# Modulation weights loaded as 64 rows by two column blocks, one partition sum per vector, and x loaded in quarters

## The chip, the cores and the metric

One core of a Trainium2 chip runs the whole program. The metric is the device time of one execution in microseconds. TensorE (PE) multiplies and transposes; VectorE (DVE), ScalarE (ACT) and GpSimd (POOL) do the rest; SyncE (SP) issues nearly all loads, which run on 16 DMA engines.

## The reference

x is 256 tokens by 1024 channels, all in float32. It goes through an encoder of two layers and then two layers of a second block, whose normalised inputs are modulated by vectors that depend on one conditioning vector c:

```python
c_silu = jax.nn.silu(c)
for layer in range(DEPTH):                                    # 2
    mods = jnp.split(c_silu @ ada_w[layer] + ada_b[layer], 9, axis=-1)
    h = modulate(rms_norm(x, norm_g[layer, 0]), mods[0], mods[1])
    x = x + 0.5 * (1 + mods[2]) * swiglu(h, ffn_w_in[layer, 0], ffn_w_out[layer, 0])
    ... # pool mixer or block attention with mods[3..5]
```

Before it, first_block: twice rmsnorm, projection w_in (1024 to 4096), neighbourhood and differential attention, gates, projection w_out, and the final norm. So there are 20 modulation vectors of 1024 (9 + 2 + 9), each the product of c_silu (1024) with a 1024x1024 slice of weights: 20 x 4 MB to be read, for one row of result each.

## The kernel before

**Weights.** The weights of the projections are cut into 189 units of 1 MB (128 partitions x 2048), in the order of use. SP loads a unit into raw (ring of RAW = 6), once unit u - 6 is used. ACT rounds it to w_hi (L647, ring of 4), DVE (L1164) or POOL (L516) computes w_lo = raw - w_hi, and PE makes three products, w_hi with the high and the low part of the activations (L1831, L1836) and w_lo with the high part (L1844), for either half t of the tokens. A step of one unit and one token half (half_step) is 12 matmuls of 512 columns. PE runs its queue in order; a step of it waits for w_hi, then for the low activations, then for w_lo.

**Modulation vectors.** They aren't made on PE's product path. A list, ada_after, fixes behind which weight unit each of N_ADA = 160 slots of 512 KB is loaded (L482) into ada_raw (ring of ADA_RING = 4); SP waits at L475 to L481 for a free slot, so the next weight unit stands behind it. DVE multiplies each 128x512 part by its column of c_silu (ccol) and adds it up (L1143, L1150, function ada, two per slot). A slot is 256 rows (2 per partition) of a 512-column half of one vector, so 4 slots make a half vector in ada_acc: a partial sum in each of 128 partitions. ada_sum (L1858) transposes it on PE in 4 blocks, and reduce_vector on DVE (L1108) sums over the free dimension; with the second half it adds the bias and finishes the vector (scale times gain, and the like). Where a sum stands is computed: in the encoder by SUM_STEPS (steps of a layer's w_in product), later behind a weight unit (sum_unit), away from two QUIET stretches; one half vector is put into the pool stage (in_pool).

**The start.** SP issues x's first token half (512 KB), the two halves of unit 0, x's second half, units 1 to 3, seven small constants, then unit 4. ACT issues the identity and the norm gains; PE, DVE and ACT all wait for both (first_in). PE makes 3 warm-up matmuls (WARM_UP), transposes x (t = 0, both halves of 512 channels), one more warm-up, and the first half step; the transposes of t = 1 stand between the low product and the w_lo product of it. On DVE and ACT, first_norm makes the high and low parts of the transposed x times the gain. ACT's first copy of an accumulator (L850) stands behind its conversion of unit 4 and the lambda constants.

**The end of an encoder layer** on DVE (L1475 on): gate, modulated parts of y, then the reductions of step 31, then fill(o + 3), which makes the low parts of the output projection's weights.

Of the kernel before, what the change touches and what calls it, by code (L numbers as in the profile page):

```python
# [50 lines left out]
ADA_RING = 4  # L51

# [8 lines left out]
WARM_UP = (3, 1)  # L61
SUM_STEPS = (5, 7, 9, 11, 12, 14, 15, 18, 22, 31)
# [133 lines left out]
def program(nc, known, x_in, w_in, w_out, ffn_in, ffn_out, pool_w, w_kv, w_q, w_o, ada_w, kv_ada_w,  # L196
# [7 lines left out]
    HALF_SLOTS = KC // 2  # L204
    N_ADA = N_VEC * 2 * HALF_SLOTS

# [10 lines left out]
    n_early = N_ADA - 2 * HALF_SLOTS  # L217
    ada_after = [int(np.searchsorted(share, (j + 0.5) / n_early)) for j in range(n_early)]
    ada_after += [first["up", 1, 1] + 3 + 2 * j for j in range(2 * HALF_SLOTS)]
# [4 lines left out]
    def half_end(v, half):  # L224

        return ada_after[(2 * v + half) * HALF_SLOTS + HALF_SLOTS - 1]

    HALVES = [(v, half) for v in range(N_VEC) for half in range(2)]
    sum_step, sum_unit, taken = {}, {}, set()
    for v, half in HALVES:  # L230
        e = half_end(v, half)
        if e < first["up", 0, 0]:
            layer = int(e >= first["in", 1])
            s = min(s for s in SUM_STEPS if s >= fill_step(e - first["in", layer]) + 2 + (e - first["in", layer] == 8) and (layer, s) not in taken)
            taken.add((layer, s))
            sum_step[layer, s] = [(v, half)]
            continue
# [3 lines left out]
        sum_unit[v, half] = e  # L241
    in_pool = max(h for h in sum_unit if sum_unit[h] < first["pool"])
    sum_unit[in_pool] = first["pool"]
    for h in range(2, len(HALVES)):
        if HALVES[h - 2] in sum_unit:
            assert sum_unit[HALVES[h - 2]] + 2 < half_end(*HALVES[h]), HALVES[h]

# [9 lines left out]
    vec_end = [sum_unit.get((v, 1), 0) + 4 for v in range(N_VEC)]  # L257

    with ExitStack() as ctx:
# [23 lines left out]
        ccol = sb("ccol", [P, 3, KC])  # L283
# [54 lines left out]
        x_in_sem = [ctx.enter_context(nc.semaphore(f"x_loaded{t}")) for t in range(NT)]  # L338
# [8 lines left out]
        first_in = ctx.enter_context(nc.semaphore("first_constants_loaded"))  # L347
# [4 lines left out]
        first_consts = [(ident[:], identity), (gcols[:], norm_cols)]  # L352
# [3 lines left out]
        N_FIRST, N_CONST = 16 * len(first_consts), 16 * len(consts)  # L356
# [42 lines left out]
        def short_work(layer, s):  # L399
            work = [("ada_reduce", half) for half in sum_step.get((layer, s - 1), [])]  # L400
# [10 lines left out]
            work += [("ada", half) for half in sum_step.get((layer, s), [])]  # L411
# [42 lines left out]
        def _(sp):  # L454
            sp.dma_start(x[:, 0, :], x_in[0:P, :]).then_inc(x_in_sem[0], 16)
            for u in range(NU):
# [13 lines left out]
                if u == 0:  # L470
                    sp.dma_start(x[:, 1, :], x_in[P:2 * P, :]).then_inc(x_in_sem[1], 16)
# [165 lines left out]
        def _(act):  # L637
# [59 lines left out]
            def norm(name, last, front=norm_front):  # L697
# [5 lines left out]
                if name == "a0":  # L703
                    act.wait_ge(first_in, N_FIRST)
# [47 lines left out]
            for into, src in first_consts:  # L752
                act.dma_start(into, src).then_inc(first_in, 16)
# [41 lines left out]
            def first_norm():  # L795
# [10 lines left out]
                act.wait_ge(first_in, N_FIRST)  # L806
                for t in range(NT):
                    act.wait_ge(*S.at("xT_done", "a0", t, 1))
# [287 lines left out]
        def _(dve):  # L1096
# [8 lines left out]
            def reduce_vector(v, half):  # L1105
                dve.wait_ge(*S.at("ada_sumT_done", v, half))
                b = job_bank["ada", v, half]
# [1247 lines left out]
```

## Time and profile before

| | |
|---|---|
| median of 3 runs | 1204.28 us (1204.13 to 1204.91) |
| the profiled execution | 1204.4 us |
| its span | 1202.0 us |
| PE busy | 1186.9 us (99%) |
| DVE, ACT, POOL busy | 799.3, 586.4, 559.0 us |
| DMA | 297.92 MB, mean 248 GB/s |
| granted TensorE clock | 1.00 of full |

The span runs from the first to the last instruction; 2.4 us lie around it. Matmuls overlap, and their ends are modelled, so PE at 99% says that PE has nearly always a matmul under way, and start-to-start distances tell what one costs. DMA shares are the time of packets over 16 engines; a full stretch shows up to about 1.04.

### The profile page before, as it was taken

What the parts mean: (1) busy time and instruction counts of PE and PEld (TensorE: products, weight loads), DVE (VectorE), ACT (ScalarE), POOL (GpSimd) and SP (SyncE); (2) the same over time, 40 slices, a digit from 0 to 9 for tenths busy, and PEclk for the clock granted to TensorE, in tenths of its full rate; (3) what the DMA queues carried; (4) which work ended last, traced back from release to release, by engine and by line L of the source; (5) the groups of instructions that cost most, each with busy time, mean ns of one, the idle gap of its engine ahead of it and who ended that gap; (6) DMA issues with size and microseconds to landing.
All of it is one profiled execution on the core that took longest, in us unless ns stands there. A gap on an engine that the chain in (4) does not pass through costs nothing.

```text
span 1202.0 us, 15430 instructions
## 1 busy us (share of the span) xinstructions
PE 1186.9 (99%) x5752; PEld 976.4 (81%) x5752; DVE 799.3 (66%) x1118; ACT 586.4 (49%) x764; POOL 559.0 (47%) x417
## 2 busy tenths in 40 slices
PE   9999999999999999999999999999999999999998
PEld 6888788788788888788888888888888887888887
DVE  6885468845786787678768666697673675644423
ACT  5566555665643443454434357444352665544440
POOL 1465334565454443545444226664452463445360
PEclk9999999999999999999999999999999999999999
DMA  9976369845798899459888748798874444766650
GB/s 352 361 272 230 106 237 336 282 161 171 240 349 293 288 352 346 158 169 340 297 309 307 275 176 283 243 332 300 305 296 166 149 156 158 262 218 203 210 192 35
DMA packets 183224, 297.92 MB, mean 248 GB/s; under 512 B 8368, under 2 KB 100208, under 8 KB 183152
## 3 DMA queue, kind: packets, MB, share of 16 engines
q1 hardware_dynamic: 177696, 284.82, 68.0%
q10 hardware_dynamic: 5456, 12.13, 2.9%
q8 instruction: 46, 0.75, 0.3%
q14 instruction: 26, 0.21, 0.1%
HBM read 295.84 MB, written 1.08 MB: 247 GB/s over the span
## 4 chain that ended last, share of the span: by engine, by line
PE 88%; DVE 5%; ACT 2%; issue 1%; SPq 1%; DMA 1%; POOL 1%; ACTq 0%; DVEq 0%
PE ps L1831 26%; PE ps L1844 26%; PE ps L1836 26%; PE ps L2097 2%; PE ps L1981 1%; PE ps L1923 1%; PE ps L1858 1%; PE ps L2009 1%; DVE w_lo L1164 1%; PE ps L1997 1%; DMA raw<-w_in 1%; POOL stat L507 1%; PE ps L1969 1%; PE ps L2020 1%; SPq L474 1%
## 5 line engine op out<-in xcount | busy, mean ns | idle before, releaser
L516 POOL TENSOR_TENSOR w_lo<-raw,w_hi 128x512 fp32r<-128x512 f32 x348 | 480.2, 1411 | 442.5 <-ACT w_hi L647 442.5
L647 ACT ACTIVATE w_hi<-raw 128x2048 fp32r<-128x2048 f32 x188 | 354.5, 1910 | 104.0 <-PE ps L1844 69.3
L1831 PE MATMUL ps<-w_hi,h_hi 128*128 128x512 f32 x1120 | 314.0, 402 | 1.1 <-issue 0.8
L1844 PE MATMUL ps<-w_lo,h_hi 128*128 128x512 f32 x1120 | 301.7, 391 | 1.8 <-DVE w_lo L1164 1.4
L1836 PE MATMUL ps<-w_hi,h_lo 128*128 128x512 f32 x1120 | 300.7, 391 | 0.0
L1164 DVE TENSOR_TENSOR w_lo<-raw,w_hi 128x2048 fp32r<-128x2048 f32 x96 | 223.7, 2334 | 110.8 <-ACT w_hi L647 108.7
L1844 PEld LDWEIGHTS ps<-w_lo,h_hi 128*128 128x128 f32 x1120 | 209.5, 188 | 49.3 <-DVE w_lo L1164 4.0
L1836 PEld LDWEIGHTS ps<-w_hi,h_lo 128*128 128x128 f32 x1120 | 210.4, 188 | 45.9 <-DVE h_lo L1225 0.2
L1831 PEld LDWEIGHTS ps<-w_hi,h_hi 128*128 128x128 f32 x1120 | 200.9, 189 | 43.7 <-issue 6.8
L1150 DVE SCALAR_TENSOR_TENSOR ps<-ada_raw,ccol,ps 128x512 f32<-128x512 f32 x240 | 181.1, 754 | 8.8 <-DMA ada_raw<-ada_w 2.0
L920 ACT ACTIVATE a_hi<-ps 128x512 fp32r<-128x512 f32 x44 | 26.4, 599 | 159.8 <-PE ps L2097 159.8
L507 POOL TENSOR_TENSOR stat<-stat,minus_half 128x1 f32<-128x1 f32 (+3 forms) x25 | 29.1, 1166 | 155.8 <-DVE stat L1201 120.2
L1831 PE MATMUL ps<-w_hi,a_hi 128*128 128x512 f32 x348 | 95.6, 397 | 0.0
L1844 PE MATMUL ps<-w_lo,a_hi 128*128 128x512 f32 x348 | 93.8, 392 | 0.0
L1836 PE MATMUL ps<-w_hi,a_lo 128*128 128x512 f32 x348 | 93.7, 391 | 0.0
L1844 PEld LDWEIGHTS ps<-w_lo,a_hi 128*128 128x128 f32 x348 | 65.4, 188 | 14.4
L1836 PEld LDWEIGHTS ps<-w_hi,a_lo 128*128 128x128 f32 x348 | 65.4, 188 | 14.3
L1831 PEld LDWEIGHTS ps<-w_hi,a_hi 128*128 128x128 f32 x348 | 64.2, 188 | 12.8
L930 ACT ACTIVATE hn<-ps 128x512 f32<-128x512 f32 x44 | 26.3, 598 | 94.0 <-PE ps L1844 94.0
L1518 DVE SCALAR_TENSOR_TENSOR hn<-hn,ps 128x512 f32<-128x512 f32 x44 | 30.2, 686 | 58.7 <-ACT hn L930 58.6
L741 ACT ACTIVATE pr<-lg,stat 128x256 f32<-128x256 f32 x64 | 31.9, 500 | 53.2 <-DVE stat L1309 53.2
L1511 DVE TENSOR_TENSOR a_lo<-ps,a_hi 128x512 fp32r<-128x512 f32 x44 | 30.4, 691 | 40.6 <-ACT a_hi L920 39.7
(198 smaller groups left out, 978.6 us busy)
## 6 DMA issues: line engine op xcount, KB each, us to landing
raw<-ffn_in SPq DMA_DIRECT2D x176, 512.0 KB, 5.7
ada_raw<-ada_w SPq DMA_DIRECT2D x144, 512.0 KB, 7.2
raw<-ffn_out SPq DMA_DIRECT2D x44, 1024.0 KB, 6.6
raw<-w_in SPq DMA_DIRECT2D x31, 1024.0 KB, 8.8
raw<-w_out SPq DMA_DIRECT2D x8, 1024.0 KB, 5.7
ada_raw<-kv_ada_w SPq DMA_DIRECT2D x16, 512.0 KB, 8.6
raw<-w_kv SPq DMA_DIRECT2D x8, 1024.0 KB, 5.6
bias<-na_bias ACTq DMA_DIRECT2D x16, 256.0 KB, 4.5
```

The source lines that it names most:

```text
L507: pool.tensor_tensor(st(at, n), st(at, n), minus_half[:, 0:n], ALU.pow).then_inc(*S.inc("rsqrt_ready", *key))
L516: ins = pool.tensor_tensor(w_lo[:, u % RAW, piece], raw[:, u % RAW, piece], w_hi[:, u % RING, piece].bitcast(F32), ALU.subtract)
L647: act.activation(w_hi[:, u % RING, :], raw[:, u % RAW, :], ACT.Copy).then_inc(*S.inc("w_hi_ready", u))
L741: ins = act.activation(pr1[:, w, t, :], lg1[:, s, t, :], ACT.Exp, bias=st(rs + 2 + t), scale=-1.0, accum_out=st(rs + t))
L920: act.activation(a_hi[:, 2 * g:2 * g + 2, :].rearrange("p k c -> p (k c)"), bank(b), ACT.Copy).then_inc(*S.inc("a_hi_ready", name, g))
L1150: ins = dve.scalar_tensor_tensor(out=into, in0=src, scalar=c, in1=acc, op0=ALU.mult, op1=ALU.add)
L1164: dve.tensor_tensor(w_lo[:, u % RAW, :], raw[:, u % RAW, :], w_hi[:, u % RING, :].bitcast(F32), ALU.subtract).then_inc(*S.inc("w_lo_dve", u))
L1511: dve.tensor_tensor(a_lo[sl].rearrange("p k c -> p (k c)"), bank(b), a_hi[sl].rearrange("p k c -> p (k c)").bitcast(F32), ALU.subtract).th ...
L1518: link(dve.scalar_tensor_tensor(out=ffn_gate, in0=ffn_tanh, scalar=1.0, in1=ps[:, b:b + 2, 0:GC], op0=ALU.add, op1=ALU.mult))
L1831: pe.matmul(bank(b), hi[:, k_in_lhs + k, tok], wh[:, k, c * 512:(c + 1) * 512], start=start and k == 0, stop=False)
L1836: pe.matmul(bank(b), lo[:, k_in_lhs + k, tok], wh[:, k, c * 512:(c + 1) * 512], start=False, stop=False)
L1844: ins = pe.matmul(bank(b), hi[:, k_in_lhs + k, tok], wl[:, k, c * 512:(c + 1) * 512], start=False, stop=stop and k == nk - 1)
```

## The change

Each slot now holds 128 rows: 64 partitions take them for the left 512 columns of the vector, 64 for the right 512, with 2 rows per partition, loaded by two DMAs of 256 KB. Eight slots make a whole vector; ada_acc then holds 64 partial sums of either half, and 4 transposes and one reduction give all 1024 sums. Slots, their sizes and the list ada_after are the same; there are 20 sums instead of 40. The columns of c_silu are laid out to match (64 rows, repeated).

```diff
+ADA_BLOCKS = 2
-WARM_UP = (3, 1)
-SUM_STEPS = (5, 7, 9, 11, 12, 14, 15, 18, 22, 31)
+WARM_UP = (2, 1)
+SUM_STEPS = (5, 7, 9, 11, 12, 14, 15, 18, 31)
...
-    HALF_SLOTS = KC // 2
-    N_ADA = N_VEC * 2 * HALF_SLOTS
+    ADA_ROWS, ADA_SET = P // ADA_BLOCKS, ADA_BLOCKS // 2
+    SLOTS, N_SETS = D // (2 * ADA_ROWS), N_VEC // ADA_SET
+    N_ADA = N_SETS * SLOTS
...
-            sp.dma_start(x[:, 0, :], x_in[0:P, :]).then_inc(x_in_sem[0], 16)
+            def load_x(t, half):
+                cols = slice(512 * half, 512 * half + 512)
+                sp.dma_start(x[:, t, cols], x_in[t * P:(t + 1) * P, cols]).then_inc(x_in_sem[t][half], 16)
+
+            load_x(0, 0)
...
                 if u == 0:
-                    sp.dma_start(x[:, 1, :], x_in[P:2 * P, :]).then_inc(x_in_sem[1], 16)
+                    for t, half in ((1, 0), (0, 1), (1, 1)):
+                        load_x(t, half)
...
-                    part, pair = divmod(j, HALF_SLOTS)
-                    w, col = vec_src[part // 2]
-                    col += 512 * (part % 2)
-                    rows = w[2 * pair * P:(2 * pair + 2) * P, col:col + 512].rearrange("(k p) n -> p k n", p=P)
-                    sp.dma_start(ada_raw[:, j % ADA_RING], rows).then_inc(ada_in[j % ADA_RING], 16)
+                    g, slot = divmod(j, SLOTS)
+                    for k in range(ADA_BLOCKS):
+                        w, col = vec_src[ADA_SET * g + k // 2]
+                        col += 512 * (k % 2)
+                        rows = w[2 * slot * ADA_ROWS:(2 * slot + 2) * ADA_ROWS, col:col + 512]
+                        sp.dma_start(ada_raw[k * ADA_ROWS:(k + 1) * ADA_ROWS, j % ADA_RING],
+                                     rows.rearrange("(i p) n -> p i n", p=ADA_ROWS)).then_inc(ada_in[j % ADA_RING], 16)
...
                 for t in range(NT):
+                    if t:
+                        fill(1)
...
-                fill(1)
+                fill(2)
                 act.wait_ge(*S.at("stat_filled"))
                 for t in range(NT):
-                    act.wait_ge(x_in_sem[t], 16)
+                    for half in range(2):
+                        act.wait_ge(x_in_sem[t][half], 16)
                     act.activation(hn[:, t, :], x[:, t, :], ACT.Square, accum_out=st(t)).then_inc(
                         *S.inc("squares_ready", "a0", t))
-                    fill(2 + t)
-                fill(4)
+                    fill(3 + t)
...
+            def reduce_set(g):
+                dve.wait_ge(*S.at("ada_sumT_done", g))
+                blocks = bank(job_bank["ada", g]).rearrange("p (k b r) -> p b k r", k=4, b=ADA_BLOCKS)
+                vectors = range(ADA_SET * g, ADA_SET * g + ADA_SET)
+                m = mods[:, ADA_SET * g:ADA_SET * g + ADA_SET, :].rearrange("p v (h k) -> p (v h) k", h=2)
+                dve.tensor_reduce(m, blocks, AX.X, ALU.add).then_inc(*S.inc("ada_reduced", g))
+                dve.wait_ge(*S.at("ada_reduced", g))
+                m, to_add = mods[:, vectors[0]:vectors[-1] + 1, :], bcols[:, vectors[0]:vectors[-1] + 1, :]
+                link(dve.tensor_tensor(m, m, to_add, ALU.add))
+                for v in vectors:
+                    finish_vector(v)
...
+                first_high(0)
+                first_low(0, 0)
+                first_high(1)
+                lows(0)
+                first_low(1, 0)
                 for t in range(NT):
                     first_low(t, 1)
-                lows(2)
+                    lows(1 + t)
...
                     low_part(("y", layer), t, 0, "yT_done")
-                for half in sum_step.get((layer, 31), []):
-                    reduce_vector(*half)
+                lows(o + 3)
+                for g in sum_step.get((layer, 31), []):
+                    reduce_set(g)
                 fill(o + 3)
...
-            reduce_vector(*in_pool)
+            reduce_set(in_pool)
...
+                for part in (range(0, nk // 2), range(nk // 2, nk)) if u == 0 and t == 0 else (range(nk),):
+                    if u == 0 and (part[0] or t):
                         pe.wait_ge(*S.at("w_hi_ready", 0))
...
+                    if u == 0 and t == 0 and part[0] == 0:
+                        raw_T(1, 0)
+                    lhs_wait(lo_ready)
...
-            pe.wait_ge(first_in, N_FIRST)
+            pe.wait_ge(ident_in, 16)
...
-                    norm_T(name, 0)
+                    raw_T(0, 0)
...
-                    if s == 0 and not layer:
-                        norm_T(name, 1)
+                    if s < 2 and not layer:
+                        raw_T(s, 1)
```

The first half step on PE is thus split in two: high and low products of the first two row blocks, with the transposes of x's quarter (1, 0) between them, then the same of the last two. raw_T(t, half) waits for one quarter of x and transposes it. ACT, DVE and the start of DVE's queue wait for the norm gains alone (gcols_in).

## Rows read from the trace of the kernel before

**Rows 1.** The page's busy times: us, share of the span, instructions.

```profile
PE 1186.9 (99%) x5752; PEld 976.4 (81%) x5752; DVE 799.3 (66%) x1118; ACT 586.4 (49%) x764; POOL 559.0 (47%) x417
```

**Rows 2.** Who PE waited for: us in total, times, longest us.

```profile
PE ps L1936 <- DVE hn L1578: 2.4, 3, 1.8
...
PE ps L1844 <- DVE w_lo L1164: 1.4, 3, 0.9
```

**Rows 3.** Stretches: us, busy of each engine, clock, DMA share, GB/s.

```profile
330.00:480.00 150.00, 150.00 (x701) 123.59 (x700) 117.95 (x138) 63.02 (x51) 67.31 (x49) 1.00 0.92 326
...
530.00:680.00 150.00, 150.00 (x700) 124.08 (x699) 118.85 (x138) 62.92 (x50) 71.50 (x52) 1.00 0.92 323
...
440.00:470.00 30.00, 30.00 (x140) 24.72 (x139) 26.17 (x29) 12.79 (x8) 15.66 (x12) 1.00 1.03 398
```

**Rows 4.** Instructions in groups: busy us, mean ns, idle before.

```profile
L1858 PE MATMUL ps<-ident,ada_acc 128*128 128x128 f32 x160 | 23.9, 272 | 0.0
...
L1108 DVE TENSOR_REDUCE mods<-ps 128x4 f32<-128x512 f32 x40 | 27.5, 688 | 1.0
```

**Rows 5.** PE's timeline around a sum: start us, us, then instruction.

```profile
338.92 1.08 PE L1844 MATMUL ps<-w_lo,h_hi 128*128 128x512 f32 x4
339.83 0.60 PE L1858 MATMUL ps<-ident,ada_acc 128*128 128x128 f32 x4
340.19 1.18 PE L1831 MATMUL ps<-w_hi,h_hi 128*128 128x512 f32 x4
...
342.12 1.07 PE L1844 MATMUL ps<-w_lo,h_hi 128*128 128x512 f32 x4
...
344.84 1.07 PE L1844 MATMUL ps<-w_lo,h_hi 128*128 128x512 f32 x4
```

**Rows 6.** Timeline of the pool stage, DVE behind the reduction [idle before].

```profile
508.62 0.69 DVE L1589 TENSOR_TENSOR h_lo<-ps,h_hi 128x512 fp32r<-128x512 f32 x1 [0.78 <-ACT h_hi L961]
```

**Rows 7.** Timeline of the output stages, layer 0 and (last row) layer 1.

```profile
139.72 0.68 DVE L1108 TENSOR_REDUCE mods<-ps 128x4 f32<-128x512 f32 x1
...
140.83 4.49 DVE L1164 TENSOR_TENSOR w_lo<-raw,w_hi 128x2048 fp32r<-128x2048 f32 x2
...
143.18 1.20 PE L1844 MATMUL ps<-w_lo,h_hi 128*128 128x512 f32 x4 [0.88 <-DVE w_lo L1164]
...
289.81 1.19 PE L1844 MATMUL ps<-w_lo,h_hi 128*128 128x512 f32 x4 [0.35 <-DVE w_lo L1164]
```

**Rows 8.** The start: one stretch as in rows 3, then the timeline.

```profile
4.00:6.00 2.00, 2.00 (x4) 0.59 (x2) 0.00 (x0) 0.00 (x0) 0.00 (x0) 1.00 1.06 390
...
7.83 0.90 PE L1831 MATMUL ps<-w_hi,h_hi 128*128 128x512 f32 x2
...
21.86 1.92 ACT L647 ACTIVATE w_hi<-raw 128x2048 fp32r<-128x2048 f32 x1 [1.63 <-DMA raw<-w_in]
...
28.36 1.07 PE L1844 MATMUL ps<-w_lo,h_hi 128*128 128x512 f32 x4
...
29.49 0.64 PEld L1969 LDWEIGHTS ps<-ident,hn 128*128 128x128 f32 x6 [0.49 <-ACT hn L850]
```

**Rows 9.** SP's issues of ada_raw (ns min/median/max), and the page's queue row.

```profile
L482 SPq DMA_DIRECT2D ada_raw<-ada_w x144: 367/470/3366, 14.7 to 1088.9; - x144
...
q1 hardware_dynamic: 177696, 284.82, 68.0%
```

**Rows 10.** DMA issues, 330 to 480 us, then 530 to 680: median us to landing.

```profile
ada_raw<-ada_w SPq DMA_DIRECT2D x28, 512.0 KB, 7.3
...
ada_raw<-kv_ada_w SPq DMA_DIRECT2D x6, 512.0 KB, 8.2
...
ada_raw<-ada_w SPq DMA_DIRECT2D x27, 512.0 KB, 7.4
...
ada_raw<-kv_ada_w SPq DMA_DIRECT2D x8, 512.0 KB, 9.4
```

**Rows 11.** Who ACT waited for: us in total, times, longest us.

```profile
ACT w_hi L647 <- DMA raw<-ffn_out: 29.1, 8, 5.9
```

More of the change, by code:

```diff
@@ L235, in program @@
             taken.add((layer, s))
-            sum_step[layer, s] = [(v, half)]
+            sum_step[layer, s] = [g]
             continue
@@ L240, in program @@
                 e = first[b] + wait + (wait > 1 and first[b] + wait in sum_unit.values())
-        sum_unit[v, half] = e
-    in_pool = max(h for h in sum_unit if sum_unit[h] < first["pool"])
+        sum_unit[g] = e
+    in_pool = max(g for g in sum_unit if sum_unit[g] < first["pool"])
     sum_unit[in_pool] = first["pool"]
-    for h in range(2, len(HALVES)):
-        if HALVES[h - 2] in sum_unit:
-            assert sum_unit[HALVES[h - 2]] + 2 < half_end(*HALVES[h]), HALVES[h]
+    for g in range(2, N_SETS):
+        if g - 2 in sum_unit:
+            assert sum_unit[g - 2] + 2 < set_loaded(g), g
     def up_sum(e):
@@ L255, in up_sum @@
         return None
-    vec_end = [sum_unit.get((v, 1), 0) + 4 for v in range(N_VEC)]
+    vec_end = [sum_unit.get(v // ADA_SET, 0) + 4 for v in range(N_VEC)]
     with ExitStack() as ctx:
@@ L337, in program @@
         bias_in = [ctx.enter_context(nc.semaphore(f"bias_in{i}")) for i in range(BIASES)]
-        x_in_sem = [ctx.enter_context(nc.semaphore(f"x_loaded{t}")) for t in range(NT)]
+        x_in_sem = [[ctx.enter_context(nc.semaphore(f"x_loaded{t}_{half}")) for half in range(2)] for t in range(NT)]
         ROWS = {("down", 0, 0): 2, "pool": 5, "pool_scale": 4, "pool_shift": 3, ("down", 0, 1): 8,
@@ L399, in short_work @@
         def short_work(layer, s):
-            work = [("ada_reduce", half) for half in sum_step.get((layer, s - 1), [])]
+            work = [("ada_reduce", g) for g in sum_step.get((layer, s - 1), [])]
             work += [("diff", h) for h in range(HEADS_DA) if DA_DIFF[h] == s]
@@ L410, in short_work @@
             work += [("da_scores", h) for h in range(HEADS_DA) if DA_SCORES[h] == s]
-            work += [("ada", half) for half in sum_step.get((layer, s), [])]
+            work += [("ada", g) for g in sum_step.get((layer, s), [])]
             return work
@@ L750, in load_bias @@
                     bias_in[i % BIASES], 16)
-            for into, src in first_consts:
-                act.dma_start(into, src).then_inc(first_in, 16)
+            act.dma_start(ident[:], identity).then_inc(ident_in, 16)
+            act.dma_start(gcols[:], norm_cols).then_inc(gcols_in, 16)
             act.wait_ge(*S.at("minus_half_ready"))
@@ L1135, in ada @@
             def ada(j):
-                part, pair = divmod(j, HALF_SLOTS)
-                dve.wait_ge(ada_in[j % ADA_RING], 16 * (j // ADA_RING + 1))
+                g, slot = divmod(j, SLOTS)
+                dve.wait_ge(ada_in[j % ADA_RING], 16 * ADA_BLOCKS * (j // ADA_RING + 1))
                 acc = bank(ADA_BANK)
                 for i in range(2):
-                    k = 2 * pair + i
-                    src, c = ada_raw[:, j % ADA_RING, i, :], ccol[:, 2, k:k + 1]
+                    k = 2 * slot + i
+                    src, c = ada_raw[:, j % ADA_RING, i, :], ccol[:, 1, k:k + 1]
                     if k == 0:
@@ L1182, in sums @@
                     u = sums_done[0]
-                    for v, half in HALVES:
-                        e = sum_unit.get((v, half), NU)
+                    for g in range(N_SETS):
+                        e = sum_unit.get(g, NU)
                         if e + 4 == u and up_sum(e) is None and e != first["pool"]:
-                            reduce_vector(v, half)
+                            reduce_set(g)
                     for j in ada_at(u):
@@ L1278, in first_low, with first_high @@
                     ins.then_inc(*S.inc("h_lo_ready", "a0", t, half))
-                for t in range(NT):
+                def first_high(t):
                     dve.wait_ge(*S.at("xT_done", "a0", t, 0))
@@ L1526, in reduce_sums @@
                 def reduce_sums(s):
-                    for v, half in HALVES:
-                        if up_sum(sum_unit.get((v, half), NU)) == (name, s):
-                            reduce_vector(v, half)
+                    for g in range(N_SETS):
+                        if up_sum(sum_unit.get(g, NU)) == (name, s):
+                            reduce_set(g)
                 for s in range(4 * NG):
```

101 lines of the change are left out of this document (45 added, 56 removed).

## The prediction

> **What bounds the kernel now.** I read the page's busy shares and its chain first, then who TensorE (PE) waits for, then the stretches in which the DMA engines are full. PE is busy for 1186.9 us of the span [rows 1], and the chain that ended last is mostly PE's matmuls. The reader should see how little PE waits: the longest sums by cause are 2.4 us in the pool stage and, at the start aside, 1.4 us for low weight parts [rows 2]. So an instruction taken out of PE's queue gives its time back, nearly everywhere, and an instruction taken out of VectorE (DVE, 799.3 us busy [rows 1]) gives nothing by itself, except at the few points where PE waits for DVE. The second limit is DMA: over two stretches of 150 us, in which PE is busy throughout, the 16 engines are 0.92 busy, and inside one of them, 440 to 470 us, they are full: 1.03 at 398 GB/s [rows 3].
>
> **Sums of the modulation vectors.** Before, every half vector is accumulated in ada_acc with one row in each of 128 partitions and summed over partitions by 4 PE transposes and one DVE reduction: 160 transposes, 40 reductions [rows 4]. After, a partition half holds one column block, and a whole vector takes 4 transposes and one reduction of the same 128x512: 80 and 20. What a group of 4 costs PE is the shift of what follows, not its busy time of 272 ns each, since matmuls overlap. From the group of low-part matmuls ahead of a sum, at 338.92 us, to the third group behind, at 342.12, it is 3.20 us; the same three groups without a sum take 344.84 - 342.12 = 2.72 us [rows 5]. A sum costs 0.48 us. Next to other transposes the second part of this (the slower first group of matmuls behind) is already paid; there it is the distance from the sum to the next group, 340.19 - 339.83 = 0.36 us [rows 5]. The 20 that go are the first halves of their vectors: by the diff's rule for the steps 5 lie in the encoder, where small transposes surround them, and 15 in the feed-forward stages. None of the places that I found by that rule is one where PE idles; the one of the pool stage stays. 15 x 0.48 + 5 x 0.36 = 9.0 us. The bounds are 20 x 0.36 = 7.2 and 20 x 0.48 = 9.6.
>
> **DVE.** The load schedule stays: 160 slots, each behind the same weight unit as before, with two multiply-adds each of the same size; a slot holds 128 rows in two column blocks instead of 256 rows in one. 20 reductions of 688 ns go [rows 4], 13.8 us off an engine that doesn't set the end. I count it at nothing, and nothing is what it costs. Reading PSUM in the new order (block, chunk, row) isn't in the trace; the reduction reads the same 512 elements per partition, and were it twice as slow, 20 x 0.7 us would land where PE doesn't wait for it. In the pool stage the reduction that stays gets the bias addition and a final operation behind it, some 0.4 us more; the next DVE instruction there idles 0.78 us for ScalarE [rows 6], which covers it; without the cover it would cost PE these 0.4 us.
>
> **Low parts ahead of the reduction, output stage.** At the end of either encoder layer DVE now makes the low weight parts first. Before, in layer 0, the reduction and two small operations stand from 139.72 to 140.83 ahead of them, and PE then idles 0.88 us for the low part; in layer 1 PE idles 0.35 us at the same place, and the reduction alone is 0.69 us [rows 4, 7]. The moved work is longer than the idle time in both, so both go: 1.2 us. The vector comes 4.5 us later, behind two low parts [rows 7], and DVE waits for PE's next product soon after, so nothing is put off by it.
>
> **The first steps.** x comes in quarters of 256 KB, so the first transposes and weights wait for 256 KB less, 0.66 us at 398 GB/s [rows 3]; one warm-up fewer and a wait for the identity alone let PE go there earlier, and the granted clock shows 1.00, so 2.4 GHz, from the first stretch on [rows 8]. The first product of 7.83 us should come 0.7 us earlier. But this isn't kept. Weight unit 4 lands at 21.86 us behind DMA engines that have been full since 4 us; ScalarE (ACT), idle 1.63 us before, converts it; then come its low part and the lambda constants on DVE, then ACT's copy of the first accumulator, and PE's transposes of that copy, which wait for it, start at 29.49 [rows 8]. None of these moves with PE: the bytes ahead of unit 4 are the same. PE's slack ahead of that point is what is to be had: the last matmul group starts at 28.36, and groups of four take 2.72 / 3 = 0.91 us [rows 5], so PE could have been there at 29.27. That is 0.2 us. Gain: 0.2 us, at most 0.9 if the landing moved too, and a loss only if PE falls behind by more than it wins, which would take a wait of over 0.7 us. The transposes of x(1,0) now stand in PE's queue between the high and the low products of the first half step; PE could wait there for that quarter, and the products behind would be late by as much. It is the fourth transfer, and 1.5 MB are ahead of and in it, 0.5 MB less than ahead of and in x's second half before, so I expect it when PE gets there, and the 0.7 us cover what remains.
>
> **DMA issue.** SyncE (SP) issues 320 half slots instead of 160 slots, and 2 more for x; an issue takes 367 ns at least, 470 at the median and 3.4 us at most [rows 9]. 160 x 0.47 = 75 us more on a queue that mostly waits for buffers to come free. The wait for a ring slot stands as before, ahead of the pair; behind it is the next weight unit, later by some 0.5 us, against a lead of over 10 us (below). Nothing, then; with the lead gone it would be 0.5 us a slot.
>
> **The price that no row shows** is that of a transfer to 64 partitions. All large loads here go to 128. Bounds from the nearest rows: at the same rate a pair costs what one slot of 512 KB costs, 1.3 us at 398 GB/s [rows 3]; at half the rate it is 1.3 us more. The nearest row has the same packets (rows of 512 columns, 2 KB) from the same weights to twice as many partitions, and nothing in the trace ties the rate of an engine to the partitions that it writes; so I take the first end and keep the second as a rival.
> The Trainium skill speaks against this change. SBUF — State Buffer, section "Door 1: The DMA port swizzle", says that 64 partitions reach only 8 of the 16 ports, measured 196 GB/s against 328 for 128 partitions at 1 MiB, and the section "Can I just issue two DMAs to hit both halves?" says that two transfers to the halves serialize. By that ratio a slot would cost 1.67 times as much, an estimate of 0.9 us more, just below the point from which rival 1 decides; no row of this case shows a 64-partition load to test it.
>
> **Sum.** 1204.4 (the profiled execution; the span 1202.0 and 2.4 around it; the median of the runs shown is 1204.28, so the same) - 9.0 - 1.2 - 0.2 = 1194.0 us.
>
> **Rival 1, slower: loads to 64 rows run at half rate.** Then each slot takes 1.3 us more of the DMA engines. The stretch 330 to 480 us has 28 + 6 = 34 slots, the one from 530 to 680 has 27 + 8 = 35 [rows 10]. They would need 45 and 46 us more, and are 0.92 busy of 1.04 possible (the most that a full stretch shows), which leaves 0.12 x 150 = 18 us. So 27 us each would be missing. The lead of the weights pays first: six raw buffers and 5.5 us per unit (two half steps of 2.72 [rows 5]) mean that a unit is asked for 27 us before its use; landing takes 7.3 us at the median for what is issued there [rows 10], conversion 1.92 [rows 8] and low part 2.2 on DVE [rows 7], more on GpSimd, which is slower; some 15 us are left. 12 us each, two stretches: 1194 + 24 = 1218 us. It decides from (18 + 15) / 34 = 1.0 us more per slot. Below that the leads hold and it costs little, between 1194 and 1198. For it speaks that ACT already waits 29.1 us in 8 places for weights of the down products, up to 5.9 us [rows 11], so the lead is thin in the full stretches. Against it, that PE waits for no load in any of them [rows 2].
>
> **Rival 2: no change.** The transposes' time comes back as new waits, since producers don't go faster: then only part (the 1.2 us of rows 7 and a few sums) is left, 1202 to 1204. Against it: PE's waits for others sum to a few us [rows 2]. This covers too that the change doesn't do what it says.
>
> **Rival 3: the start goes through.** If the landing of unit 4 moves with the quarters, 0.7 us more: 1193.3.
>
> **Chances.** Forecast with rival 3, and rate losses below the turning point: 0.66, own range 1191.0 to 1198.5 (all sums at 0.48 and the start through: 1192.7, and a little less if DVE's relief counts somewhere; up to 4 us of rate losses). Rival 1 beyond it: 0.25, from 1200 to 1222, most near 1210 to 1218. Rival 2: 0.09. The range goes from 1191.0 to 1213.0; above are some 0.14 of rival 1. About 0.2% (2.4 us) is what a measurement of this kernel can tell from no change; faster by more: 0.67; within: 0.08; slower: 0.25.
>
> **What would show it.** Right: 80 transposes of ada_acc and 20 reductions; PE's idle time for the low part gone in both output stages; the first product near 7.1 us but the transposes behind the first evacuation still near 29.4; queue q1 at the share of before, 68.0% [rows 9]. Wrong: q1's share at 80 to 86%, DMA at 1.0 throughout both 150 us stretches, PE or DVE waiting for raw or ada_raw there, and a difference that appears after 330 us. If instead the start is late, the wait is PE's for x ahead of 12 us.

## The result, and the profile after

| | before | after |
|---|---|---|
| median | 1204.28 us | 1323.78 us (1316.72 to 1338.39, 4 runs) |
| ratio | | 1.097, interval 1.094 to 1.100 |
| profiled execution, span | 1204.4, 1202.0 us | 1338.39, 1336.3 us |
| granted TensorE clock, mean | 1.00 | 0.967 |

By these medians the changed kernel is 119.5 us slower. The forecast was 1194.0 us, the top of its range 1213.0: wrong in sign and far outside. The profiled execution of after, 1338.39 us, is the longest of its four and counts as a slow run, so the ratio leaves it out (the median of the other three is 1318.81 us), and the rows below are read for where time goes, not for the last per cent.

The page of after: busy shares, two queues, two kinds of DMA issue (KB each, median us to landing), and the chain that ended last by engine; these answer to [rows 1, 9, 10].

```profile
PE 1222.7 (91%) x5670; PEld 987.5 (74%) x5670; DVE 781.7 (58%) x1098; ACT 589.2 (44%) x764; POOL 543.5 (41%) x417
...
q1 hardware_dynamic: 180544, 284.83, 82.2%
...
PE 37%; DMA 37%; DVE 13%; SPq 7%; ACT 3%; issue 2%; POOL 1%; ACTq 0%; DVEq 0%
...
ada_raw<-ada_w SPq DMA_DIRECT2D x288, 256.0 KB, 11.4
```

PE idles for 1336.3 - 1222.7 = 113.6 us, against 15.1 before; that is 98 us of the loss. The rest is in the busy time: it grew by 35.8 us although 80 transposes are gone. Most of this is the clock, whose mean over the span is 0.967 where it was 1.00; some 5 us are an effect of addresses that comes below. The queue q1 moved the same 284.8 MB as before, and was in transfer for 0.822 x 1336.3 = 1098 us instead of 0.680 x 1202.0 = 817 [rows 9]: 281 us more, 1.76 us for each of 160 slots. The only other edit of a transfer is x in quarters, 1 MB in all, so this row already points at the loads of the slots. Whether it is their number, their size or their partitions, it can't say.

Stretches of after (columns as in [rows 3]), two of them those of [rows 3], and one of the encoder:

```profile
330.00:480.00 150.00, 134.98 (x605) 108.90 (x604) 95.19 (x113) 63.73 (x64) 56.71 (x43) 0.97 1.02 244
...
440.00:470.00 30.00, 25.17 (x108) 20.36 (x107) 17.12 (x21) 10.27 (x10) 10.22 (x8) 0.89 1.08 233
30.00:130.00 100.00, 86.58 (x449) 69.49 (x450) 58.27 (x133) 50.65 (x108) 45.72 (x37) 0.97 1.03 261
```

The DMA engines are as full as they ever were in 440 to 470 us (1.08; before 1.03), and move 233 GB/s where they moved 398 [rows 3]. A share of 1.0 with the rate down by 40% means that the packets themselves take longer, not that there is more to move. And the loss begins at once: PE is busy for 87 of 100 us from 30 us on.

Who waited for whom in after (us in total, times, longest):

```profile
PE ps L2121 <- DVE hn L1541: 52.1, 15, 10.6
PE ps L1866 <- DVE w_lo L1178: 8.8, 5, 5.0
...
DVE ps L1164 <- DMA ada_raw<-ada_w: 186.1, 82, 6.5
ACT w_hi L655 <- DMA raw<-ffn_in: 138.4, 36, 7.2
ACT w_hi L655 <- DMA raw<-ffn_out: 127.4, 26, 8.7
```

PE's greatest wait isn't for weights. It is for hn, the gated activation of the feed-forward stage, from DVE. The timeline of after around the longest of these shows why; a last row gives the stretch 484 to 498 us as a whole:

```profile
488.24 1.91 ACT L655 ACTIVATE w_hi<-raw 128x2048 fp32r<-128x2048 f32 x1 [7.50 <-DMA raw<-ffn_out]
490.40 0.75 DVE L1157 TENSOR_SCALAR ps<-ada_raw,ccol 128x512 f32<-128x512 f32 x1 [6.56 <-DMA ada_raw<-ada_w]
...
492.81 1.55 DVE L1164 SCALAR_TENSOR_TENSOR ps<-ada_raw,ccol,ps 128x512 f32<-128x512 f32 x2 [0.86 <-DMA ada_raw<-ada_w]
494.39 0.69 DVE L1530 TENSOR_TENSOR a_lo<-ps,a_hi 128x512 fp32r<-128x512 f32 x1
...
495.71 0.69 DVE L1541 TENSOR_TENSOR hn<-ps,hn 128x512 f32<-128x512 f32 x1
...
496.46 1.12 PE L2121 MATMUL ps<-ident,hn 128*128 128x128 f32 x4 [10.61 <-DVE hn L1541]
```

```profile
484.00:498.00 14.00, 3.39 (x14) 2.41 (x13) 6.57 (x8) 2.30 (x2) 0.60 (x1) 0.63 1.04 252
```

DVE's queue is in order, and the multiplications for the next vector stand ahead of the activation. DVE waits 6.56 us for a slot, then 0.86 for the next, with a_lo and hn behind it, and PE waits 10.61 us for hn. ACT's wait for raw runs at the same time. So the modulation slots have no lead of their own any more, and their lateness reaches PE through DVE. With PE idle, the granted clock is 0.63 in this stretch, a mean between its levels of 1.2 and 2.4 GHz. The matmuls behind the wait pay for that again: the first group of four below starts 1.86 us ahead of the next, where groups stand 0.93 us apart at full clock.

```profile
497.22 2.06 PE L1851 MATMUL ps<-w_hi,a_hi 128*128 128x512 f32 x4
499.08 1.91 PE L1858 MATMUL ps<-w_hi,a_lo 128*128 128x512 f32 x4
```

### The profile page after: what moved, and what is told of

It reads as the page before. It is cut to its first block, busy times and chain, and to the rows that moved or that the text cites. A ratio compares the mean times of both kernels' runs of the same rounds, so it can differ in the third digit from the quotient of the medians.

```text
span 1336.3 us, 15370 instructions
## 1 busy us (share of the span) xinstructions
PE 1222.7 (91%) x5670; PEld 987.5 (74%) x5670; DVE 781.7 (58%) x1098; ACT 589.2 (44%) x764; POOL 543.5 (41%) x417
## 3 DMA queue, kind: packets, MB, share of 16 engines
q1 hardware_dynamic: 180544, 284.83, 82.2%
HBM read 295.84 MB, written 1.08 MB: 222 GB/s over the span
## 4 chain that ended last, share of the span: by engine, by line
PE 37%; DMA 37%; DVE 13%; SPq 7%; ACT 3%; issue 2%; POOL 1%; ACTq 0%; DVEq 0%
DMA ada_raw<-ada_w 29%; PE ps L1866 11%; PE ps L1851 11%; PE ps L1858 11%; SPq L489 5%; DMA ada_raw<-kv_ada_w 5%; DVE ps L1164 4%; DMA bias<-na_bias 3%; DVE w_lo L1178 2%; SPq L473 2%; PE ps L1945 1%; ACT w_hi L655 1%; PE ps L2033 1%; DMA raw<-w_in 1%; POOL stat L515 1%
## 5 line engine op out<-in xcount | busy, mean ns | idle before, releaser
L524 POOL TENSOR_TENSOR w_lo<-raw,w_hi 128x512 fp32r<-128x512 f32 x348 | 463.3, 1363 | 603.0 <-ACT w_hi L655 603.0
L1164 DVE SCALAR_TENSOR_TENSOR ps<-ada_raw,ccol,ps 128x512 f32<-128x512 f32 x280 | 211.5, 755 | 210.1 <-DMA ada_raw<-ada_w 186.1
L1851 PE MATMUL ps<-w_hi,h_hi 128*128 128x512 f32 x1120 | 318.0, 406 | 1.0 <-issue 1.0
L1858 PE MATMUL ps<-w_hi,h_lo 128*128 128x512 f32 x1120 | 306.0, 395 | 0.0
L1851 PEld LDWEIGHTS ps<-w_hi,h_hi 128*128 128x128 f32 x1120 | 205.1, 192 | 45.2 <-issue 7.0
L1866 PE MATMUL ps<-w_lo,a_hi 128*128 128x512 f32 x348 | 99.4, 409 | 9.0 <-DVE w_lo L1178 8.8
L1851 PE MATMUL ps<-w_hi,a_hi 128*128 128x512 f32 x348 | 100.3, 411 | 4.0 <-ACT w_hi L655 4.0
L1858 PE MATMUL ps<-w_hi,a_lo 128*128 128x512 f32 x348 | 99.3, 408 | 0.0
L2121 PE MATMUL ps<-ident,hn 128*128 128x128 f32 x176 | 30.1, 298 | 58.5 <-DVE hn L1541 52.1
L2121 PEld LDWEIGHTS ps<-ident,hn 128*128 128x128 f32 x176 | 22.1, 150 | 69.0 <-DVE hn L1541 66.0
## 6 DMA issues: line engine op xcount, KB each, us to landing
raw<-w_in SPq DMA_DIRECT2D x31, 1024.0 KB, 15.1
ada_raw<-kv_ada_w SPq DMA_DIRECT2D x32, 256.0 KB, 10.6
```

Of the source, the lines that this page charges most:

```text
L524: ins = pool.tensor_tensor(w_lo[:, u % RAW, piece], raw[:, u % RAW, piece], w_hi[:, u % RING, piece].bitcast(F32), ALU.subtract)
L1164: ins = dve.scalar_tensor_tensor(out=into, in0=src, scalar=c, in1=acc, op0=ALU.mult, op1=ALU.add)
L1851: pe.matmul(bank(b), hi[:, k_in_lhs + k, tok], wh[:, k, c * 512:(c + 1) * 512], start=start and k == 0, stop=False)
L1858: pe.matmul(bank(b), lo[:, k_in_lhs + k, tok], wh[:, k, c * 512:(c + 1) * 512], start=False, stop=False)
L1866: ins = pe.matmul(bank(b), hi[:, k_in_lhs + k, tok], wl[:, k, c * 512:(c + 1) * 512], start=False, stop=stop and k == nk - 1)
L2121: ins = pe.transpose(bank(b)[:, c * T + t * P:c * T + (t + 1) * P], ffn_act[:, g % 2, t, c * P:(c + 1) * P], ident[:])
```

## The experiments

### Two transfers per slot, over 128 partitions

```diff
-                    sp.dma_start(ada_raw[:, j % ADA_RING], rows).then_inc(ada_in[j % ADA_RING], 16)
+                    for i in range(2):
+                        sp.dma_start(ada_raw[:, j % ADA_RING, i:i + 1], rows[:, i:i + 1]).then_inc(ada_in[j % ADA_RING], 16)
```

> The kernel before, with each slot of modulation weights loaded by two DMAs of 256 KB to all 128 partitions (one row of 2 KB per partition each): the number, size and packets of the DMAs are those of the changed kernel, the partitions those of before. Theory A (the loads are slow because they go to 64 partitions): no change, 1203 to 1206 us, q1 at 68%. Theory B (the loads are slow because there are twice as many, half as large, or because SyncE issues twice as often): near 1324 us or above, since the sums of before stay.

Measured: 1204.35 us, ratio to before 1.0002 (0.9993 to 1.0012). Twice as many issues of half the size cost nothing.

### Two transfers per slot, to the halves of the partitions

The kernel before, with `part = slice(64 * i, 64 * i + 64)` and `sp.dma_start(ada_raw[part, j % ADA_RING], rows[part])` in the same place. Same slots, same data, 40 sums as before.

> The kernel before, with each slot loaded by two DMAs to the partition halves 0 to 63 and 64 to 127, both rows of each partition in one: only the destination of a DMA differs from e1_two_by_row. Theory A: the loss of the changed kernel and the sums of before, 1320 to 1345 us, q1 at 80 to 83% of the longer span. Theory B: the same time as e1_two_by_row, near 1324 us as well. If neither slows, the loss comes from the source side, from two column blocks of the same rows: 1204 us for both.

Measured: 1323.37 us, ratio 1.099 (1.096 to 1.102), as slow as the changed kernel (1.094 to 1.100). Its page and its waits show the same picture:

```profile
q1 hardware_dynamic: 180256, 284.83, 82.0%
```

```profile
PE ps L2099 <- DVE hn L1524: 48.0, 15, 9.6
```

What this kernel and the changed one share against before is two transfers per slot and the halves, and two transfers cost nothing. So the halves are the whole loss, as far as four runs each with a spread of 8 and 22 us can tell.

PE's instructions are those of the kernel before, so its groups can be laid side by side. The same group in before and here, behind the encoder and where the loss has ended:

```profile
329.79 1.08 PE L1844 MATMUL ps<-w_lo,h_hi 128*128 128x512 f32 x4
353.30 1.08 PE L1846 MATMUL ps<-w_lo,h_hi 128*128 128x512 f32 x4
...
891.41 1.07 PE L1836 MATMUL ps<-w_hi,a_lo 128*128 128x512 f32 x4
1012.09 1.07 PE L1838 MATMUL ps<-w_hi,a_lo 128*128 128x512 f32 x4
```

PE is 23.5 us late at 330 us of the kernel before, 57.4 at 511, 95.3 at 714 and 120.7 at 891, and that is what it stays at to the end. So the encoder loses 23.5 us, the stretches from 330 to 511 and from 511 to 714 us lose 34 and 38, and the one from 714 to 891 another 25.

### The changed kernel with even and odd partitions

```diff
-                        sp.dma_start(ada_raw[k * ADA_ROWS:(k + 1) * ADA_ROWS, j % ADA_RING],
+                        sp.dma_start(ada_raw[k::ADA_BLOCKS, j % ADA_RING],
...
-                blocks = bank(job_bank["ada", g]).rearrange("p (k b r) -> p b k r", k=4, b=ADA_BLOCKS)
+                blocks = bank(job_bank["ada", g]).rearrange("p (k r b) -> p b k r", k=4, b=ADA_BLOCKS)
```

The columns of c_silu are laid out to match. A transfer still writes 64 partitions with 2 rows of 512 columns, but every second one.

> The changed kernel, with the left column block on the even and the right one on the odd partitions, instead of on the lower and the upper 64; sum and columns of c_silu are laid out to match. Same number of DMAs, same 64 rows in each. Theory A in its form by halves (what is slow is a transfer that stays within one half of the partitions): the loss goes and the forecast holds, 1192 to 1197 us, q1 at 68%. Theory A in its form by count (any transfer to 64 partitions is slow) and theory B: 1310 to 1340 us as before.

Measured: 1200.41 us, ratio 0.997 (0.996 to 0.998), and q1 is at the old share:

```profile
q1 hardware_dynamic: 180544, 284.83, 68.7%
```

So it isn't the number of 64 partitions that costs, but that they lie in one half. This kernel beats both, yet it gains 3.6 us where the forecast's sum has 10.4. The rest of the study is about these 7 us, and about the price of the halves.

### Loads alone

> Leaves out all of the computation and returns x: only loads, in eight segments with a full stop between them, 12 slots of 512 KB each: (1) whole slots to 128 partitions, (2) two DMAs by row to 128, (3) two to the halves, (4) two to even and odd partitions, (5) the left column block alone to the lower half (256 KB each), then 8 weight units of 1 MB alternating with (6) whole slots, (7) slots by halves, (8) slots by even and odd. Theory A by halves: about 390 GB/s in 1, 2, 4, 6 and 8, half of it, 195 to 220, in 3 and 5, and in 7 the time of 6 plus 8 x 1.3 us if a slot by halves costs twice as much, plus 8 x 2 us if it costs what the changed kernel shows (see its 7.1 us per unit with 1.25 slots, against 2.9 us for the unit alone, so 3.3 us a slot). Theory B: 2 and 4 as slow as 3.

The kernel computes nothing. Windows within its segments (us, POOL, clock, DMA share, GB/s): whole slots; slots as halves; unit and whole slot; unit and slot as halves; unit and slot as even and odd. A unit is the 1 MB of weights.

```profile
4.00:14.00 10.00, 0.00 (x0) 1.00 1.04 391
...
40.00:58.00 18.00, 0.00 (x0) 1.00 1.04 239
...
108.00:134.00 26.00, 0.00 (x0) 1.00 1.05 389
146.00:186.00 40.00, 0.00 (x0) 1.00 1.06 243
198.00:224.00 26.00, 0.00 (x0) 1.00 1.05 389
```

With halves alone the rate falls from 391 to 239 GB/s: 2.2 us per slot of 512 KB, 0.85 more than whole. The issues at which the three mixed segments begin, and the next, are at 105.22, 140.81, 195.43 and 230.74 us: 35.6, 54.6 and 35.3 us for 8 units and 8 slots. In the mix a slot as halves costs (54.6 - 35.6) / 8 = 2.4 us more. The weights are slow there too: a third of the 2 KB packets between 146 and 186 us are the slots', but 71% of all take over 105 ns, against 2% with whole slots alone. Even and odd cost nothing.

The Trainium skill, SBUF — State Buffer, sections "Door 1: The DMA port swizzle" and "Can I just issue two DMAs to hit both halves?", says that one half of the partitions reaches 8 of 16 ports and that two such transfers serialize; here whole and halves stand at 391 and 239 GB/s, 0.61, and the page's 196 to 328 is 0.60. By that rule the slot costs 0.9 us more, and the run of halves alone agrees. Its figure doesn't hold for the mix, which measured 2.4.

### Mixes

> Loads alone again, nothing is computed and the output is x; six stretches one after the other, each waits for the end of the last. (1) 8 weight units of 1 MB; (2) 8 x (unit, then 256 KB to the lower 64 partitions); (3) 8 x (lower half slot, unit, upper half slot); (4) 8 units, then 8 slots as pairs of halves; (5) 4 x (2 units, 2 slots as halves); (6) 8 units from SP's queue and 8 slots as halves from ScalarE's at the same time. In the mix of before (unit, slot as halves) the queue moved 250 GB/s throughout, 6.3 us per unit and slot. Additive reading: a unit costs 2.7 us and a slot as halves 2.2, wherever they stand; then (4) takes 39 us as well as (3), (5) and (6), and the 6.3 us were something else. Reading that mixing itself costs: (4) takes 39 us and (3) some 50, (2) more than 8 x (2.7 + 1.1) = 30 us, and (5) lies between.

The first issue of each segment behind the first, from the timeline of SP's queue (one row each), and x at the end:

```profile
25.26 0.37 SPq L25 DMA_DIRECT2D wide<-w_in  x1
...
67.09 0.60 SPq L25 DMA_DIRECT2D slots<-ada_w  x1
...
115.36 2.45 SPq L25 DMA_DIRECT2D wide<-w_in  x4
...
158.22 0.93 SPq L25 DMA_DIRECT2D wide<-w_in  x2
...
205.67 1.56 SPq L25 DMA_DIRECT2D wide<-w_in  x3
...
251.01 0.81 SPq L25 DMA_DIRECT2D x<-x_in  x2
```

Segment 1 starts at 0.73 us, so the six take 24.5, 41.8, 48.3, 42.9, 47.5 and 45.3 us. Taking off the 24.5 of eight units alone, a slot as halves costs 2.3 us when all come behind the units (segment 4), 2.6 from another queue (6), 2.9 when two units and two slots alternate (5), 3.0 with the unit between the halves (3), and 3.8 as unit, lower, upper (the run before: (54.6 - 24.5) / 8), which is the order of the changed kernel. A lower half alone, 256 KB, costs 2.2 beside each unit (2), where the rate of 239 would give 1.1 (lower halves alone, in the run before, went at some 215 GB/s, so 1.2). A whole slot costs 1.4. So the additive reading falls: alternation between wide and half transfers costs up to 1.5 us a cycle on top. Of the reading that mixing itself costs, segments 2 and 5 came as said and segment 3, with some 50 us, at 48.3; but segment 4, for which both readings said 39 us, took 42.9. What it is in the engines that makes alternation dear, and why the order of the halves matters, stays open.

### The start alone

The kernel before with all edits of the first steps (x in quarters, the split first half step, the waits for identity and gains apart, ACT's and DVE's new order, WARM_UP) and nothing else.

> The kernel before with the edits of the first steps alone: x in quarters, the split first half step, the waits for identity and gains apart, one warm-up fewer. Forecast's reading: 0.2 us faster, 1204.1 to the 1204.3 of before. Reading from the even/odd kernel, whose transposes behind the first evacuation stand 1.0 us later than before although its first product is earlier: the start costs time, 1205.3, and the shift of +1.0 us at those transposes is here too, with no later jump.

Measured: 1205.32 us against 1203.69, ratio 1.001 (1.0001 to 1.0019): slower by 1.6 us between the medians, 1.2 by the ratio, with an interval that nearly reaches zero. The timeline of this run shows where: SP's issue of x's three other quarters, then of units from unit 4 on, ACT's conversion of unit 4, and PE's transposes behind the first evacuation.

```profile
2.16 1.42 SPq L457 DMA_DIRECT2D x<-x_in  x3
...
13.14 2.66 SPq L472 DMA_DIRECT2D raw<-w_in  x2
...
22.45 1.92 ACT L652 ACTIVATE w_hi<-raw 128x2048 fp32r<-128x2048 f32 x1 [1.00 <-DMA raw<-w_in]
```

```profile
8.52 0.66 PE L1937 MATMUL ps<-ident,x 128*128 128x128 f32 x4 [1.31 <-DMA x<-x_in]
...
30.08 1.09 PE L1985 MATMUL ps<-ident,hn 128*128 128x128 f32 x8 [0.93 <-ACT hn L857]
```

The first product is at 6.51 us, 1.3 earlier than before; PE then waits 1.31 us for x's quarter (1, 0). Unit 4 is converted at 22.45 instead of 21.86 us, and the transposes stand at 30.08 instead of 29.50 [rows 8]. SP has two issues more ahead, and unit 4 was issued at 12.66 us in the kernel before. The bytes ahead of it are the same, SP's work isn't. The DMA share and rate from 4 to 22 us, before and here:

```profile
4.00:22.00 18.00, 17.34 (x74) 12.38 (x73) 13.25 (x23) 11.91 (x18) 4.31 (x3) 1.00 1.06 386
4.00:22.00 18.00, 16.34 (x74) 12.08 (x73) 11.78 (x23) 11.99 (x17) 2.71 (x3) 1.00 1.04 373
```

The difference, 13 GB/s over 18 us or 0.23 MB, is worth 0.6 us, as much as unit 4 is late. It agrees with SP's later issues as the cause; that it isn't the smaller packets of x in quarters was not tested apart.

### The address of the activations

In the even/odd kernel I aligned PE's records with those of the kernel before. It stands 0.3 to 0.6 us earlier behind every place where a sum is gone, as forecast, but gives back 0.07 us in every four groups on a_hi and a_lo, in all feed-forward down products. Those groups have nothing in common with the change except that ccol grew from 24 to 32 floats, which moves whatever is allocated behind it by 32 bytes.

```diff
         ccol = sb("ccol", [P, 3, KC])
+        pad = sb("pad", [P, 8])
```

The same line with 8 floats in the kernel before and in the even/odd kernel, and with 16 in the kernel before:

> The kernel before with an unused buffer of 8 floats (32 bytes per partition) behind ccol, so that everything allocated behind it lies 32 bytes further, a_hi and a_lo (the activations of the down products) among them; nothing else changes. In the changed kernel and in the even/odd one ccol itself is 32 bytes larger (32 floats for 24). Theory: in the even/odd kernel the matmul groups on a_hi and a_lo stand 0.018 us further apart each (0.073 us in four), and the address is why: some 265 groups of four, 4.8 us, so 1209.1, with the a_hi/a_lo rows at 395 ns for 392 and those on h_hi unchanged. Rival: the larger distance comes from something else of that kernel (the loads, DVE's order); then this is 1204.3.

> The even/odd kernel with the same unused 8 floats behind ccol, which put a_hi and a_lo at 64 bytes beyond their place in the kernel before. Theory of the address: the 32 bytes were what costs, and at 64 the 4.8 us come back: 1200.4 - 4.8 = 1195.6, a_hi/a_lo rows at 392 ns. Rival, something else of the even/odd kernel slows them: 1200.4 as it was. Second rival, any shift from the old place costs: 1200.4 or more.

> The kernel before with an unused buffer of 16 floats (64 bytes per partition) behind ccol. On a_hi and a_lo the groups of four stand 0.915 us apart in the kernel before, 0.933 with 32 bytes more, and 0.907 in the padded even/odd kernel, whose a_hi lies 64 bytes beyond its old place; groups on h_hi stand 0.907 apart everywhere. Theory: this is the address alone, three levels of it, so here too 0.907, 264 groups x 0.008 = 2.1 us less: 1201.6 against 1203.7, and a_hi/a_lo rows at 389 ns. Rival: the third level belongs to the even/odd kernel; then 1203.7.

Measured: 32 bytes in the kernel before, 1208.08 against 1203.69 us, ratio 1.004 (1.003 to 1.005). 32 more in the even/odd kernel: 1193.94, ratio 0.992 (0.991 to 0.993), 6.5 us below the even/odd kernel without it. 64 bytes in the kernel before: 1202.15 against 1204.1, ratio 0.998 (0.997 to 0.999). Groups on PE in a down product, each pair three groups apart, first the kernel before, then 32 bytes, then 64 bytes further (start us, us):

```profile
455.69 1.08 PE L1836 MATMUL ps<-w_hi,a_lo 128*128 128x512 f32 x4
...
458.43 1.08 PE L1836 MATMUL ps<-w_hi,a_lo 128*128 128x512 f32 x4
```

```profile
457.04 1.09 PE L1845 MATMUL ps<-w_lo,a_hi 128*128 128x512 f32 x4
...
459.84 1.09 PE L1845 MATMUL ps<-w_lo,a_hi 128*128 128x512 f32 x4
```

```profile
456.05 1.07 PE L1845 MATMUL ps<-w_lo,a_hi 128*128 128x512 f32 x4
...
458.77 1.07 PE L1845 MATMUL ps<-w_lo,a_hi 128*128 128x512 f32 x4
```

Three groups take 2.74, 2.80 and 2.72 us: 0.913, 0.933 and 0.907 each. Over all of them the first is 0.915 (0.913 on a_lo, 0.916 on a_hi). There are 264 groups on a_hi and a_lo, so 32 bytes cost 4.8 us against before and 64 bytes give back 2.1; measured 4.4 and 2.0. From the allocation sizes, a_hi starts at 151232 + 16384 bytes plus whatever lies below the first buffer: an odd multiple of 64 before, if that base is a multiple of 128, which nothing here shows; with the 64 bytes more it is a multiple of 128, with 32 it is neither. h_hi, whose groups go at 0.907 in every kernel, starts at a multiple of 128 by the same count. The rivals, by which the spacing comes from something else in the even/odd kernel or any shift costs, fall. For the padded even/odd kernel I had forecast 1195.6, because I took the place of the kernel before as the best one; it is the middle one of three.

### The sums with the old start

The padded even/odd kernel with the start of the kernel before: one sum per vector and the low parts first.

> The padded even/odd kernel with the start of the kernel before (x in halves, three warm-ups and one), so one sum per vector and the low parts ahead of the reduction alone. If the start's edits cost 1.0 us and the address 4.8: 1194.6. If the start costs nothing in the end: 1195.6. If the address isn't the cause either: 1199.4.

Measured: 1193.13 us, ratio 0.991 (0.990 to 0.993), the fastest of all, 10.6 us below the 1203.69 beside it. PE's idle times for the low part are gone. Two places take time back. The timeline of this run on DVE in the pool stage, and at the end of encoder layer 1:

```profile
501.27 0.68 DVE L1114 TENSOR_REDUCE mods<-ps 128x8 f32<-128x512 f32 x1
...
501.99 0.52 DVE L1117 TENSOR_TENSOR mods<-mods,bcols 128x8 f32<-128x8 f32 x1
...
502.54 1.20 DVE L1133 TENSOR_SCALAR mods<-mods 128x8 f32<-128x8 f32 x1
```

```profile
288.89 1.22 DVE L1139 TENSOR_SCALAR mods<-mods 128x8 f32<-128x8 f32 x1
...
291.47 2.20 DVE L1500 TENSOR_TENSOR hn<-x,row 128x1024 f32<-128x1024 f32 x1
...
297.42 1.09 PE L1932 MATMUL ps<-ident,hn 128*128 128x128 f32 x8 [0.71 <-ACT hn L890]
```

In both places a half vector ended before, with the reduction alone; now a whole one ends there and is finished. Its last operation on 128x8 elements takes 1.2 us while GpSimd makes low parts. The line of the second has seven instances in the kernel before (L1131 there): six take 0.17 us, with GpSimd idle, and one takes 1.26, beside GpSimd's pieces of 1.26 us each:

```profile
239.29 3.78 POOL L516 TENSOR_TENSOR w_lo<-raw,w_hi 128x512 fp32r<-128x512 f32 x3 [4.24 <-ACT w_hi L647]
239.33 1.26 DVE L1131 TENSOR_SCALAR mods<-mods 128x8 f32<-128x8 f32 x1
```

The operation ends with the piece that it meets, so it seems to wait for it. hn<-x,row, which meets GpSimd in both kernels, ends 1.08 us behind the piece that is under way at its start, and takes 2.20 us in place of 1.61 because it starts earlier in such a piece. PE falls back by 1.1 us behind 300 us and by 1.2 us in the pool stage.

### The low parts alone

`lows(o + 3)` ahead of the reductions of step 31, in the kernel before.

> The kernel before with the low weight parts ahead of the reduction in both output stages, nothing else. Forecast's reading: both idle times go, 1.2 us: 1202.5. Reading from the even/odd kernels: PE stands 1.0 us earlier behind 143 us and 0.5 us earlier behind 290 us, but at 301 us, at the transposes that wait for the normalised x, 0.8 us of it is lost again, since the chain through DVE and ScalarE ahead of them hasn't become faster: 1203.7 - 1.5 + 0.8 = 1203.0, and a wait of PE for ScalarE's hn near 300 us.

Measured: 1202.29 us against 1204.10, ratio 0.999 (0.998 to 0.9996). In its timeline PE gains 1.1 us at 143 us and 0.6 more at 290. The loss that I had put at 301 us isn't there; that place gives time back only with a whole vector finished ahead of it, so it belongs to the run above. The profiled execution, 1203.48 us, is the longest of the eleven: it gives back 0.8 us in the pool stage, where nothing was changed. So of the 1.2 us there in the run above, not all need be the finished vector.

## Why the prediction was wrong, point by point

**A transfer to 64 partitions: the step that failed.** The text had both ends, the same rate and half of it, and took the first because the nearest row writes twice as many partitions with the same packets and "nothing in the trace ties the rate of an engine to the partitions that it writes". That no row shows a tie is not evidence of none: all rows had 128 partitions. It also put the rule of the Trainium skill, which named this case, in a sentence that changed nothing, though by it a slot costs 0.9 us more and rival 1 decides from 1.0. Measured: 0.85 alone, 2.4 in the mix, 1.76 as the mean over the changed kernel.

**Rival 1 had the mechanism and a fifth of the size** (24 us above the forecast, measured 130). Its end of 1.3 us was no bound, since it priced the slot as if alone; the queue is slowed in the weights too. With 2.4 us its own sum reads (34 + 35) x 2.4 - 2 x (18 + 15) = 100 us, so 1294. But the loss doesn't lie there alone. By the run with halves the two stretches gave 34 + 38 = 72 us, and the encoder (23.5) and the stretch from 714 to 891 us (25), for which the rival counted nothing, gave the rest. Of what it said would show, q1's share (82.2%), DMA at 1.0 and waits for ada_raw came; "appears after 330 us" didn't, and 530 to 680 us is not full throughout. It looked for the lateness at the weights, with their lead of 15 us. The first to be late are the slots, which DVE meets in its own queue ahead of hn. The falling clock was in no case; 1222.7 x (1 - 0.967) = 40 us is an estimate of it, somewhat high, since the mean clock covers PE's idle time too.

**The sums: right.** Of the 10.6 us of the kernel with the old start, 1.7 are the low parts and 2.0 the address, and 2.3 were given back at two places; so the 20 sums are worth 10.6 - 1.7 - 2.0 + 2.3 = 9.2 us by difference. Forecast: 9.0, bounds 7.2 and 9.6. 80 transposes and 20 reductions are there. That is a difference of five terms and carries their errors, a few tenths each.

**The low parts: right and a little more**, 1.7 us by the trace for 1.2.

**DVE at nothing: wrong in one place.** The forecast priced the finishing operations at 0.4 us and let 0.78 us of idle time cover them [rows 6]. They take 1.7 us there, beside GpSimd, and PE loses 1.2 us, of which some may have another cause (the low parts alone). The second place, the end of layer 1, was not looked at for this.

**The start: the sign was wrong.** Forecast a gain of 0.2 us with the landing of unit 4 unmoved; it moved by 0.6 us the other way. The forecast counted bytes ahead of unit 4 and left out SP's issues, though it had counted them for the slots; that they are the cause is likely, not shown. "If the start is late, the wait is PE's for x ahead of 12 us" named a true wait (1.31 us), but that one is absorbed; the late landing isn't.

**Nothing of the address was in the forecast**: 32 bytes in ccol, visible in the diff, cost what half of the sums gain.

**Together** the even/odd kernel reads 9.2 - 4.8 + 1.7 - 2.3 - 1.0 = 2.8 us of gain, measured 3.6. The padded one comes to 1193.94, the forecast 1194.0 but for the halves; that it agrees is luck: 2 us of address make up for losses that the forecast lacked.

## What to carry to other kernels

When an edit narrows a transfer, ask which partitions it writes, not only how many, and give the worse price the weight until a row or a load-only run of the very mix decides. In this kernel every second partition loads like all of them, so a layout by blocks can be had without the halves. And any edit that changes the size of one buffer moves the others: compare the spacing of matmul groups by operand before crediting or blaming the edit.

## What the runs showed of the hardware

- Transfers to partitions 0 to 63 or 64 to 127 go at 239 GB/s where whole ones reach 391 (in the mix 389, and even/odd ones too), and when they alternate with 128-partition transfers, those are slowed too: 2.4 us more per 512 KB in place of 0.85.
- Matmul groups go at 0.907, 0.915 or 0.933 us per four, by whether the stationary operand lies at a multiple of 128, of 64 or of 32 bytes, as worked out from the allocation sizes. Only three offsets were tried.
- An operation of DVE on 128x8 elements takes 1.2 us when it meets a piece of GpSimd's low parts, and ends with that piece; of the seven at the same line (L1131) of the kernel before, the six that meet none take 0.17.
- A wait of PE costs twice: in the stretch where PE waits 10.6 us, its clock is 0.63, and the group of four behind the wait takes 1.86 us in place of 0.93.
